# Two layer norms: ScalarE adds the bias and makes the next input from the scaled tile, in place of VectorE

## What is computed

```python
def layernorm(x, g, b):
    mu = xf.mean(-1, keepdims=True)
    var = jnp.square(xf - mu).mean(-1, keepdims=True)
    return (xf - mu) * lax.rsqrt(var + LN_EPS) * g + b

for i in range(2):                       # first block
    shift, scale, gate = split(silu(c) @ ada_w[i] + ada_b[i], 3)
    u = x * (1 + scale) + shift
    y = mixer_i(u)
    x = layernorm(ALPHA * x + gate * y, ln_g[i], ln_b[i])
...
hn = _rms(x, g[0])                       # second block, first layer: x * rsqrt(mean(x*x) + EPS) * g
```

## Time and profile before

| | |
|---|---|
| timed runs, median (range of 3) | 2786.96 us (2786.29 to 2789.31) |
| the profiled execution, its own time | 2789.52 us |
| its span, first to last instruction | 2787.7 us |
| mean granted TensorE clock | 0.997 |
| instructions | 37044 |
| PE busy | 2747.7 us, 99% |
| DVE busy | 1330.0 us, 48% |
| ACT busy | 939.1 us, 34% |
| POOL busy | 1234.6 us, 44% |
| first norm, from PE's column sums to the end of the opening | about 344 to 376 us |
| second norm, the same | about 624 to 660 us |

### The profile page before, as it was taken

How to read it: one execution, slowest core, us unless ns; L and a number is a source line. 1 busy time by engine, 2 the same in 40 slices (tenths; PEclk the granted TensorE clock), 3 DMA queues, 4 the chain that set the end, 5 groups by cost and what they waited for, 6 DMA issues and landing times.

```text
span 2787.7 us, 37044 instructions
## 1 busy us (share of the span) xinstructions
PE 2747.7 (99%) x13800; PEld 2281.1 (82%) x13800; DVE 1330.0 (48%) x1825; ACT 939.1 (34%) x1318; POOL 1234.6 (44%) x913
## 2 busy tenths in 40 slices
PE   9999999999999999999999999999999999999997
PEld 6888877887888888888888888878888888888886
DVE  4344675668455441175441276565441174544413
ACT  4443447743133222252222334342222221422222
POOL 4445332134535545515555443235454454454554
PEclk9999999999999999999999999999999999999999
DMA  9655231122323333313333321223333333233332
GB/s 329 160 184 190 76 121 54 32 61 76 98 76 106 98 97 99 115 66 112 93 97 104 99 89 59 61 62 112 98 98 103 102 91 91 83 106 97 91 107 97
DMA packets 106251, 285.09 MB, mean 102 GB/s; under 512 B 38733, under 2 KB 38861, under 8 KB 104851
## 3 DMA queue, kind: packets, MB, share of 16 engines
q1 hardware_dynamic: 99488, 258.33, 30.8%
q10 hardware_dynamic: 6643, 25.05, 2.5%
HBM read 281.08 MB, written 8.85 MB: 104 GB/s over the span
## 4 chain that ended last, share of the span: by engine, by line
issue 41%; PE 34%; POOL 23%; DVE 1%; POOLq 0%; ACT 0%; DMA 0%; ACTq 0%
POOL w_lo L647 23%; PE ps L450 11%; PE ps L452 11%; PE ps L451 11%; PE ps L514 0%; DVE x L2558 0%; DVE tmp L2552 0%; POOLq L645 0%; PE ps L503 0%; POOLq L166 0%; PE ps L732 0%; PE ps L754 0%; DMA par<-in_cols 0%; PE ps L531 0%; PE ps L498 0%
## 5 line engine op out<-in xcount | busy, mean ns | idle before, releaser
L647 POOL TENSOR_TENSOR w_lo<-w_raw,w_hi 128x512 fp32r<-128x512 f32 x904 | 1233.7, 1388 | 1542.3 <-ACT w_hi L443 1542.3
L450 PE MATMUL ps<-u_hi,w_hi 128*128 128x512 f32 x2256 | 885.9, 393 | 9.5 <-DVE u_lo L2301 6.5
L452 PE MATMUL ps<-u_hi,w_lo 128*128 128x512 f32 x2256 | 879.0, 390 | 0.0
L451 PE MATMUL ps<-u_lo,w_hi 128*128 128x512 f32 x2256 | 878.6, 389 | 0.0
L443 ACT ACTIVATE w_hi<-w_raw 128x1024 fp32r<-128x1024 f32 x452 | 475.2, 1055 | 778.6 <-PE ps L452 741.5
L450 PEld LDWEIGHTS ps<-u_hi,w_hi 128*128 128x128 f32 x2256 | 423.9, 188 | 105.0 <-DVE u_lo L2301 10.5
L452 PEld LDWEIGHTS ps<-u_hi,w_lo 128*128 128x128 f32 x2256 | 423.8, 188 | 88.9
L451 PEld LDWEIGHTS ps<-u_lo,w_hi 128*128 128x128 f32 x2256 | 424.1, 188 | 88.1 <-issue 1.9
L450 PE MATMUL ps<-h_hi,w_hi 128*128 128x512 f32 (+1 forms) x726 | 277.9, 383 | 0.0
L452 PE MATMUL ps<-h_hi,w_lo 128*128 128x512 f32 (+1 forms) x726 | 277.8, 383 | 0.0
L451 PE MATMUL ps<-h_lo,w_hi 128*128 128x512 f32 (+1 forms) x726 | 277.7, 383 | 0.0
(11 more groups left out here) (342 smaller groups left out, 3010.1 us busy)
## 6 DMA issues: line engine op xcount, KB each, us to landing
w_raw<-in_stream SPq DMA_DIRECT2D x452, 512.0 KB, 3.6
late_ring<-in_ada_late ACTq DMA_DIRECT2D x32, 512.0 KB, 5.7
ada_ring<-in_ada SPq DMA_DIRECT2D x8, 1024.0 KB, 17.4
dilated_bias_rows<-dilated_bias SPq DMA_DIRECT2D x18, 244.1 KB, 4.7
band_a<-dilated_bias_rows SPq DMA_DIRECT2D x96, 28.0 KB, 2.0
x<-in_x SPq DMA_DIRECT2D x8, 256.0 KB, 17.5
bias_rows<-bias_scratch ACTq DMA_DIRECT2D x4, 512.0 KB, 7.6
out_yT<-x SPq DMA_DIRECT2D x8, 256.0 KB, 2.0
```

The lines of the kernel that those rows point to most:

```text
L450: nc.tensor.matmul(o, w[0], v[0], start=start, stop=False)
L451: nc.tensor.matmul(o, w[0], v[1], start=False, stop=False)
L452: return nc.tensor.matmul(o, w[1], v[0], start=False, stop=stop)
L647: ins = nc.gpsimd.tensor_tensor(w_lo[:, s, half], w_raw[:, s, half], w_hi[:, s, half].bitcast(F32), ALU.subtract)
```

## The change

In both norms the bias leaves DVE. A bias column for the next input's high part is worked out ahead, on DVE, into `den[:, 0, :]` (layer 0: ln_b x (1 + scale) + shift; layer 1: ln_b x next gain). The scaling signals `ln_v` and is not waited for on DVE itself. ACT waits for `ln_v`. Layer 0: it makes `u_hi` and `tmp` from the scaled x with the new column, then adds the bias to x in place. Layer 1 (`normed_parts`, new): it reads the scaled tile three times through the rearranged view, for `u_hi`, for x (with the bias) and for the square (with the bias), and writes in natural order. The scaled tiles have a ring of three (two of `tmp`, and `rs`); from the fourth on the scaling waits for the square of three tiles before. DVE's low part in layer 1 now waits for `x_done` of ACT as well as for `u_hi`. DVE keeps per tile: mean, scaling, low part (and the additions of squares).

```diff
+    def norm_tile(t):
+        return (tmp[:, 2, :], tmp[:, 3, :], rs[:, :])[t % 3].rearrange("p (r b a) -> p a b r", r=4, b=4)
+
+    def by_token(tile):
+        return tile.rearrange("p (a b r) -> p a b r", b=4, r=4)
...
             def ada_parts():
 
+                act.wait_ge(ln_bias, 1)
                 for t in range(KD):
-                    act.wait_ge(x_done, n.up("xd"))
+                    act.wait_ge(ln_v, t + 1)
                     if t >= 2:
                         act.wait_ge(u_ready, KD + t - 1)
                     for dst in (u_hi[:, t, :], tmp[:, t % 2, :]):
                         nc.scalar.activation(dst, x[:, t, :], ACT.Identity, scale=mod[:, 32 + t:33 + t],
-                                             bias=mod[:, 24 + t:25 + t]).then_inc(u_hi_ready, 1)
+                                             bias=den[:, 0, t:t + 1]).then_inc(u_hi_ready, 1)
+                    b0 = COLS["ln_b"] + t
+                    n.up("xd")
+                    nc.scalar.activation(x[:, t, :], x[:, t, :], ACT.Identity,
+                                         bias=par[:, b0:b0 + 1]).then_inc(x_done, 1)
...
                 if next_scaled is not None:
-                    scaled_parts(*next_scaled)
-
-            def x_square_to_add(t):
+                    normed_parts(layer, *next_scaled)
+
+            def normed_parts(layer, scaled_layer, which):
+
+                act.wait_ge(ln_bias, layer + 1)
+                for t in range(KD):
+                    act.wait_ge(ln_v, KD * layer + t + 1)
+                    g0, b0 = norm_col(scaled_layer, which, t), COLS["ln_b"] + 8 * layer + t
+                    nc.scalar.activation(by_token(u_hi[:, t, :]), norm_tile(t), ACT.Identity, scale=par[:, g0:g0 + 1],
+                                         bias=den[:, 0, t:t + 1]).then_inc(u_hi_ready, 1)
+                    n.up("xd")
+                    nc.scalar.activation(by_token(x[:, t, :]), norm_tile(t), ACT.Identity,
+                                         bias=par[:, b0:b0 + 1]).then_inc(x_done, 1)
+                    x_square_to_add(t, norm_tile(t), par[:, b0:b0 + 1])
+
+            def x_square_to_add(t, src=None, bias=0.0):
...
-                nc.scalar.activation(x_square_tile(t) if t else acc[:, :], x[:, t, :], ACT.Square).then_inc(sq_ready, 1)
+                dst = x_square_tile(t) if t else acc[:, :]
+                if src is None:
+                    src = x[:, t, :]
+                else:
+                    dst = by_token(dst)
+                nc.scalar.activation(dst, src, ACT.Square, bias=bias).then_inc(sq_ready, 1)
...
             def layernorm(layer, nxt_scaled):
+                ln_b = par[:, COLS["ln_b"] + 8 * layer:COLS["ln_b"] + 8 * layer + KD]
+                if nxt_scaled is None:
+                    ch(nc.vector.tensor_tensor(den[:, 0, :], ln_b, mod[:, 32:32 + KD], ALU.mult))
+                    nc.vector.tensor_tensor(den[:, 0, :], den[:, 0, :], mod[:, 24:24 + KD], ALU.add).then_inc(ln_bias, 1)
+                else:
+                    g0 = norm_col(nxt_scaled[0], nxt_scaled[1], 0)
+                    nc.vector.tensor_tensor(den[:, 0, :], ln_b, par[:, g0:g0 + KD], ALU.mult).then_inc(ln_bias, 1)
...
+                squares = n.get("sq", 0)
                 for t in range(KD):
-                    g0, b0 = COLS["ln_g"] + 8 * layer + t, COLS["ln_b"] + 8 * layer + t
-                    v = x[:, t, :] if nxt_scaled is None else tmp[:, 2 + t % 2, :]
-                    ch(nc.vector.scalar_tensor_tensor(out=v, in0=x[:, t, :], scalar=par[:, g0:g0 + 1],
-                                                      in1=bank(5), op0=ALU.mult, op1=ALU.mult))
+                    g0 = COLS["ln_g"] + 8 * layer + t
+                    v, src, factor = x[:, t, :], x[:, t, :], bank(5)
                     if nxt_scaled is not None:
-                        v = v.rearrange("p (r b a) -> p a b r", r=4, b=4)
-                        next_parts(nxt_scaled, t)
-                    ins = nc.vector.tensor_scalar(x[:, t, :], v, par[:, b0:b0 + 1], None, ALU.add)
-                    ins.then_inc(x_done, 1)
-                    n.up("xd")
-                    if nxt_scaled is None and t:
-                        first_lo(t - 1)
+                        v = (tmp[:, 2, :], tmp[:, 3, :], rs[:, :])[t % 3]
+                        if t >= 3:
+                            dve.wait_ge(sq_ready, squares + t - 2)
+                    nc.vector.scalar_tensor_tensor(out=v, in0=src, scalar=par[:, g0:g0 + 1], in1=factor, op0=ALU.mult,
+                                                   op1=ALU.mult).then_inc(ln_v, 1)
+                    if t:
+                        n.up("xd")
+                        if nxt_scaled is None:
+                            first_lo(t - 1)
+                        else:
+                            dve.wait_ge(x_done, n["xd"])
+                            next_parts(nxt_scaled, t)
                     if t + 2 < KD:
                         less_rest_mean(t + 2)
+                n.up("xd")
                 if nxt_scaled is None:
                     first_lo(KD - 1)
                     n.up("u", KD)
                     dve.wait_ge(u_ready, n["u"])
-                next_parts(nxt_scaled, KD)
+                else:
+                    dve.wait_ge(x_done, n["xd"])
+                    next_parts(nxt_scaled, KD)
```

More of the change, by code:

```diff
@@ L362, in build @@
     ln_spread = sem("norm_factor_spread")
+    ln_v = sem("norm_scaled_tile_ready")
+    ln_bias = sem("norm_bias_of_parts_ready")
     sqx_ready = sem("x_squares_ready")
```

## The result

| | before | after |
|---|---|---|
| median of 22 runs each | 2788.22 us | 2792.01 us |
| range | 2786.29 to 2789.86 | 2789.71 to 2793.42 |
| the profiled execution: time, span | 2789.52, 2787.7 | 2792.68, 2790.9 |

The ratio is 1.0014, with a 95% interval of 1.0008 to 1.0019: slower, by a little. The forecast was 2782.8, faster by 0.15%, with a range up to 2787.4. Sign and range were both wrong.

What follows compares the result with a forecast made beforehand. PE, busy 99% of the time, bounds the kernel, so only its waits can pay. Gains of 0.75 + 0.6 + 2.8 = 4.15 us take the median from 2786.96 to 2782.8 us, range 2780.3 to 2787.4.

Steps and rivals of the forecast that it cites:

- First norm, DVE and ACT: First norm: PE starts 0.75 us earlier as the bias leaves DVE; ACT takes 2.07 us a tile, under PE's 2.7.
- The unknown cost: ACT reading the second norm's scaled tile with a step of 512 bytes: taken as nothing; from above 0.43 us an instruction.
- The prediction's own signs of being wrong: Wrong if: ACT back to back, DVE waiting for x in every tile, a PE wait at the sum, new low clock.
- Rival A: Second norm: ACT pays for the step and becomes the bound; 2790.8 us at 0.43 us an instruction; chance 0.12.
- p: Second norm: extra us for each of ACT's three reads with a step; x 7 ends at 647.0 + 23p.
- the base of 647.0: Second norm: time in us when x 7 ends and low part 7 starts if p is nothing.
- Second norm, head and rest: Second norm: PE starts 0.6 us earlier (head); three later waits go, 2.8 us, 3.7 if matmuls quicken too (rest).
- Rival B: Behind the first norm: with shorter PE idle time the low clock, 1.65 us, may stay away, giving 2781.1; chance 0.17.
- The base: Whole kernel before the change: the median of three timed runs, 2786.96 us, from which the gain was taken.

Runs made afterwards that it cites:

- e1: The first norm as in the changed kernel, the second norm as in the kernel before: 2786.89 us, ratio 0.9994.
- e8: The kernel before without the reordering behind the second norm, so VectorE's bias reads without a step: 2785.35 us in one execution.
- e6: The changed kernel, but VectorE reorders the tokens in the subtraction of the rest of the mean and ScalarE reads without a step: 2783.57 us, ratio 0.9985.
- e3: The changed kernel without the reordering in the second norm, so ScalarE reads and writes without a step: 2782.97 us, ratio 0.9980.
- e7: The changed kernel with 18 in place of 10 dummy matmuls behind the second norm's factor: 2792.43 us, ratio 1.0016.
- e9: The changed kernel, but ScalarE's view swaps whole blocks of 32 tokens, innermost step 4 bytes: 2782.41 us in one execution.
- e12: e6 with 16 in place of 10 dummy matmuls behind the second norm's factor: 2783.01 us, ratio 0.9980.
- e2: The first norm as in the kernel before, the second norm as in the changed kernel: 2792.16 us, ratio 1.0015.
- e5: The changed kernel, but ScalarE reads with the step once, for x, and makes high part and square from x: 2784.89 us, ratio 0.9988.

## Why the prediction was wrong, by its own steps

- **First norm, DVE and ACT.** Right. High part right behind the scaling, PE's idle time 1.15 us (said: 1.1), gain 0.7 in the profile (said: 0.75), ACT 2.03 us a tile (2.07). Going against the rule of the Trainium skill ("ScalarE: Activation LUTs") that sends adds to VectorE costs nothing here, as said: ACT has the time, and its bias is 0.71 us of a tile's 2.03. By whole runs only the disappearance of before's upper heap is seen: e1's median is where before's lower heap is. Why the lower heap of before is not 0.7 above e1 stays open: the heaps are 2.6 us apart and the low clock in the profile cost 1.6, and no execution of the lower heap was profiled.
- **The unknown cost. This is the step that failed.** "I take nothing, by the DVE row." The row compared 0.67 us with VectorE's other operations and read it as one element a cycle with no fine on top. But without the step the same instruction takes 0.48 (e8), and another VectorE operation with the same step goes from 0.68 to 1.1 (e6). The row was no evidence for another engine, and hardly for its own. The measured price on ScalarE is 0.43 to 0.55 us, about 0.5 in the mean, at and just above the upper bound of 0.43 that rested on ScalarE's own rows for 512 and 1024 elements. Between ends far apart I chose by a row of another engine, when the only rule that speaks of such reads (the Trainium skill, "SBUF — State Buffer") spoke for the other end. I gave it 0.12. The prediction's own signs of being wrong came: ACT back to back with DVE waiting for x in every tile, and a low clock in the second opening that was not there before.
- **Rival A, its arithmetic.** Right in kind. By its formula the sum comes 4.5 us late at p = 0.43, and 5.9 late at the 0.49 that ScalarE's round shows ((3.41 - 1.94) / 3, from e3's round to the changed kernel's); the data were 3.9 late. The nearness of 4.5 and 3.9 is luck. Two terms were too long: the base of 647.0 is VectorE's path, which no longer counts once ScalarE is the bound (ScalarE's own, 630.95 + 7 x 1.98 + 1.44, ends at 646.25), and the additions behind the last low part were taken as before (from that low part to the copy 5.26 us, now 4.29). It left out that longer idle times bring the clock down: PE was 5.3 late, 1.4 of it clock. The chance of a slower kernel within 0.2% was there, but the range ended at 2787.4, below A's own 2790.8.
- **Second norm, head and rest.** Right where the step is absent. e3: from the column sums to the first product 9.31 us against 9.86 (gain 0.55, said 0.6); from there to the sum 20.52 against 24.01 (gain 3.5, said 2.8, with 3.7 as its end). The term was too small because the 90 matmuls also came down, from 0.236 us each to 0.228. The prediction had this as its upper end (3.7) and did not expect it, since the list of waits does not show it.
- **Rival B, the clock.** The fall behind the first norm is absent from every profiled execution with the shorter idle time (after, e1, e3 to e7, e9 to e12, 1.14 or 1.15 us each). With the longer one it is a matter of chance: before, e2 and e8 have the same first norm and idle times of 1.84, 1.83 and 1.83 us, and the clock fell in the first two and not in e8. The heaps of before go with it: over the timed runs of before beside the experiments, all 12 with a mean granted clock of 0.998 lie at 2787.6 or below, and all six with 0.996 at 2788.7 or above. Where in the run the clock fell in those, and what makes up the 1 us by which the heaps are further apart than one such fall, is not shown.
- **The base.** The median of three was the lower heap's. Over 22 runs it is 2788.2. This moved nothing in the sign.

## What to carry to other kernels

Before an operation moves to another engine, look at the innermost step of what it reads and writes: at 16 and at 512 bytes from one float32 element to the next, each such read of ScalarE took 0.5 us longer for 512 elements, and 8 bytes cost next to nothing. If an order must be changed, change it once, in one instruction, on the engine that has time, and let all others read the result (e5, e6, e12); that turned the same idea from 0.14% slower into 0.12 to 0.2% faster. And a wait that starves PE for 2 us can be paid again in clock when PE itself sets the pace behind it, though not while it is starved anyway (e7, e12). In the two openings of the profiled executions the clock fell behind every one of PE's idle times of 2.10 us or more, behind three of the eight between 1.83 and 2.05, and behind none of 1.7 or less.

## What the runs showed of the hardware that was not expected

- ScalarE, 128x512 float32: 707 ns in order, 746 at a step of 8 bytes, 1195 at 16, 1204 at 512 (x with a bias column). The step on the write side, 64 bytes, costs about the same per instruction (1173 ns), but neighbouring instructions overlap by 0.2 us and not by 0.1.
- VectorE, 128x512: bias with one tensor source 0.48 in order and 0.67 at 512 bytes; subtraction with a second source in PSUM 0.68 and 1.1.
- ScalarE's instructions with a step got longer once PE's products ran, x from 1.14 us for the first tile to 1.26 for the seventh; without the step they stayed at 0.71. The last tile's, made while PE waited, took 1.18 again. Whether they compete with PE, and for what, was not tried.
